# Per-turn interleaving, split first products and an earlier table preload in a chunked RWKV-7 recurrence

## The reference, cut to what matters

```python
def step(state, inp):
    r_t, w_t, k_t, v_t, kk_t, a_t = inp
    sa = jnp.einsum('bhvk,bhk->bhv', state, -kk_t)
    state = (state * w_t[:, :, None, :]
             + sa[..., None] * (kk_t * a_t)[:, :, None, :]
             + v_t[..., None] * k_t[:, :, None, :])
    return state, jnp.einsum('bhvk,bhk->bhv', state, r_t)
...
o = ((o - mean) * lax.rsqrt(var + GN_EPS)).reshape(B_, S, D) * gn_w + gn_b
bonus = jnp.sum(r * k * r_k, axis=-1, keepdims=True) * v
o = (o + bonus.reshape(B_, S, D)) * jax.nn.silu(g)
return o.astype(x.dtype) @ w_o
```

## Time and profile before

| | us |
|---|---|
| median of 3 runs | 2659.07 |
| lowest and highest of them | 2655.52, 2662.23 |
| profiled execution, its own time | 2662.23 |
| its span in the profile | 2660.4 |

### The profile page before, as it was taken

One profiled execution on the slowest core, in us unless ns is written; L12 is line 12 of the kernel. 1 busy time (PEld: TensorE's weight loads), 2 busy tenths in 40 slices (PEclk: granted clock), 3 DMA queues, 4 the chain that ended last, 5 costly groups with the idle time before them and its releaser, 6 DMA issues.

```text
span 2660.4 us, 38077 instructions
## 1 busy us (share of the span) xinstructions
PE 2508.1 (94%) x15424; PEld 2163.3 (81%) x15424; DVE 1568.4 (59%) x2116; ACT 1174.1 (44%) x1547; POOL 71.4 (3%) x92
## 2 busy tenths in 40 slices
PE   7999999998999999999997999999899989998786
PEld 6888888887788888888886888878788878876575
DVE  5888887765656566654446566654516662444455
ACT  5444554644444444443343464643553101444544
POOL 0000000000000000000000000000002110111000
PEclk9999999999999999999999999999999999998898
DMA  6554555554356565565554555545534564222352
GB/s 217 186 190 155 163 173 184 167 185 155 119 182 190 180 191 188 186 191 185 186 183 143 182 162 190 163 135 162 186 98 133 165 194 164 77 73 72 131 167 87
DMA packets 419535, 428.21 MB, mean 161 GB/s; under 512 B 25360, under 2 KB 414480, under 8 KB 418400
## 3 DMA queue, kind: packets, MB, share of 16 engines
q1 hardware_dynamic: 415312, 404.90, 47.8%
q0 software_dynamic: 4048, 20.88, 2.3%
HBM read 415.46 MB, written 10.22 MB: 160 GB/s over the span
## 4 chain that ended last, share of the span: by engine, by line
PE 77%; DVE 13%; ACT 5%; DMA 2%; issue 2%; SPq 0%; POOL 0%; ACTq 0%; DVEq 0%
PE GP L1745 69%; PE SB L1745 7%; DVE wL L982 4%; ACT wH L487 2%; DVE acc L988 1%; DVE y L982 1%; DMA raw<-w_gate_up_dram 1%; DVE j L982 1%; DVE x L982 1%; DVE f L988 0%; DVE ga L982 0%; DMA raw<-w_in_dram 0%; DVE Xs L1448 0%; DVE T L982 0%; DMA gv<-g_keep 0%
## 5 line engine op out<-in xcount | busy, mean ns | idle before, releaser
L982 DVE TENSOR_TENSOR wL<-raw,wH 128x1024 fp32r<-128x1024 f32 x664 | 805.3, 1227 | 618.7 <-ACT wH L487 617.6
L487 ACT CAST wH<-raw 128x1024 fp32r<-128x1024 f32 x664 | 683.9, 1048 | 575.1 <-PE GP L1745 326.1
L1745 PE MATMUL GP<-u2B,wH 128*128 128x512 f32 x1408 | 496.8, 397 | 0.0
L1745 PE MATMUL GP<-uB,wH 128*128 128x512 f32 x1152 | 409.4, 399 | 0.0
L1745 PE MATMUL GP<-u2B,wL 128*128 128x256 f32 x1408 | 398.5, 283 | 10.4 <-DVE u2B L988 8.0
L1745 PE MATMUL GP<-uB,wL 128*128 128x256 f32 x1152 | 329.5, 286 | 15.4 <-DVE wL L982 15.4
L1745 PEld LDWEIGHTS GP<-u2B,wH 128*128 128x128 f32 x1408 | 265.3, 188 | 62.2
L1745 PEld LDWEIGHTS GP<-u2B,wL 128*128 128x128 f32 x1408 | 267.1, 190 | 15.4 <-issue 8.1
L1745 PE MATMUL GP<-xB,wH 128*128 128x512 f32 x768 | 271.4, 395 | 0.0
L1745 PEld LDWEIGHTS GP<-uB,wH 128*128 128x128 f32 x1152 | 217.7, 189 | 52.1
L1745 PE MATMUL GP<-hB,wH 128*128 128x512 f32 x704 | 245.1, 392 | 0.0
(11 more groups left out here) (393 smaller groups left out, 3270.4 us busy)
## 6 DMA issues: line engine op xcount, KB each, us to landing
raw<-w_gate_up_dram SPq DMA_DIRECT2D x352, 256.0 KB, 3.6
raw<-w_in_dram SPq DMA_DIRECT2D x288, 256.0 KB, 3.4
raw<-ev_w_in_dram SPq DMA_DIRECT2D x192, 256.0 KB, 3.3
raw<-w_down_dram SPq DMA_DIRECT2D x176, 256.0 KB, 3.3
raw<-w_out_dram SPq DMA_DIRECT2D x64, 256.0 KB, 3.6
raw<-ev_w_out_dram SPq DMA_DIRECT2D x64, 256.0 KB, 3.3
dw<-w_k_dram SPq DMA_DIRECT2D x64, 256.0 KB, 3.2
dw<-w_r_dram SPq DMA_DIRECT2D x64, 256.0 KB, 3.3
```

Of the source, the lines that this page charges most:

```text
L487: e.copy(wH[SLOT[i]], raw[m % RAW].rearrange("p (k n) -> p k n", k=4)).then_inc(s["hi"], 1)
L982: return e.tensor_tensor(o, a, b, op)
L1745: return e.matmul(o, l, r, start=start, stop=stop, skip_group_check=True)
```

## The change

Three edits are made in four places. The turns are placed one by one: turn t follows the pair at which t / 0.69 is passed, counted anew for every eight units (44 turns each). In a norm on ScalarE the table preload moves from stage 3, ahead of the Ln, to stage 0, ahead of the wait for VectorE and of the Square. In a job's stage 0 on TensorE, eight products of 128 weight columns by 128 moving columns, alternating between the two halves of the partitions, become sixteen of 64 moving columns: for h = 0 four with the 128-wide pair against `rh` and four with `ka` alone (64 wide) against `al`, then the same for h = 1. The product of `be` with `al` is no longer made. In stage 4 the eight products are the same, ordered by h first and then by j.

```diff
         def turns_behind(u):
 
-            t0 = 8 * (u - U0["w_g"])
-            return [3 * (int((t + 1) * FINE / 3) - int(t * FINE / 3)) for t in range(t0, t0 + 8)]
+            t0 = 8 * ((u - U0["w_g"]) % 8)
+            return [int((t + 1) * FINE) - int(t * FINE) for t in range(t0, t0 + 8)]
 
         def turn_at(u):
-            return 3 * int(8 * (u - U0["w_g"]) * FINE / 3)
+            full, t0 = (u - U0["w_g"]) // 8, 8 * ((u - U0["w_g"]) % 8)
+            return full * int(64 * FINE) + int(t0 * FINE)
...
             def norm(k, n, c, h):
                 p0, a0, d0, _ = BASE[k][n]
                 o_, q = rh[:, 8 * h:8 * h + 8, 64 * c:64 * c + 64], fl(sets[k]["M34"].rearrange("p j h t -> p (j h) t"))
+                e.preload_act_table_set("natural_log_exp_and_others")
                 yield
                 e.wait_ge(s[f"jd{k}"], d0 + 1)
                 e.activation(q.rearrange("p (j t) -> p j t", j=8), o_, ACT.Square).then_inc(s[f"ja{k}"], 1)
                 yield
                 yield
-                e.preload_act_table_set("natural_log_exp_and_others")
...
-
-                for j in range(4):
-                    for h, b in enumerate((b0, b1)):
-                        ins = mm(b.rearrange("p (w j t) -> p w j t", w=2, j=4)[:, :, j, :],
-                                 both_[half(h), 4 * (4 * g + j) + c, :], wide[half(h), 5:7, 4 * g + j, cs], True, True)
+                for h, b in enumerate((b0, b1)):
+                    for j in range(4):
+                        mm(b[:, 64 * j:64 * j + 64], both_[half(h), 4 * (4 * g + j) + c, :], rh[half(h), 4 * g + j, cs], True, True)
+                    for j in range(4):
+                        ins = mm(b[up, 256 + 64 * j:320 + 64 * j], ka[half(h), 4 * (4 * g + j) + c, :],
+                                 al[half(h), 4 * g + j, cs], True, True)
                 ins.then_inc(jp, 1)
...
-                for j in range(4):
-                    for h, b in enumerate((b0, b1)):
+                for h, b in enumerate((b0, b1)):
+                    for j in range(4):
                         ins = mm(b[0:64, 64 * j:64 * j + 64], X[half(h), 16 * g + 4 * j + c, :], U0_[half(h), j, :], True, True)
```

## The result

The changed kernel takes 2728.57 us (median of 4 runs, 2722.53 to 2731.47) against 2659.27 us: ratio 1.0259, 95% interval 1.0236 to 1.0281, so about 69 us slower. The forecast was 2711 us with a range up to 2728. The profiled execution took 2725.73 us, with a span of 2723.9, 63.5 more than before.

What follows compares the result with a forecast made beforehand. TensorE bounds the `w_g` stretch (207.8 of 235 us busy). 38.4 stage 0 + 7.5 stage 4 + 8.9 turns + 4.8 preload - 8.0 filled waits = 51.6 us; 2662.2 becomes 2713.8, less 3.2 for the median: 2711 us, range 2686 to 2728.

Steps and rivals of the forecast that it cites:

- the stretch: Stretch of `w_g`, 235 us, the only one the change touches: some 52 us longer, all else the same.
- stage 0: TensorE's products at a job's start: 3.40 us a job against 1.00, so 38.4 us more in 16 jobs.
- One record a step: Stage 0 on TensorE: halves no longer run side by side; steps 0.112 us for 128-wide records, 0.058 for others.
- rival (a): Stage 0: 128-column loads hide behind 64 moving columns, so it costs 23.4 us, not 38.4; time 2696; chance 0.20.
- rival (b): Stages 0 and 4: loads don't overlap with one half at work; steps 0.165 and 0.111 us; time 2751; chance 0.06.
- Rival (c): TensorE: halves still run together and all 22 us of waits go, so not slower: 2660 or 2651; chance 0.06.
- 3.8 us in the last round: ScalarE, round 7: three norms each pay 1.28 us more of table load, nothing hides it, cast 3.8 us later.
- rival (d): ScalarE: the moved preload costs in every round, 12.9 us rather than 1; time 2723; chance 0.06.
- X: Stage 4 on TensorE: eight steps of two records become sixteen of one, 0.47 us a job, 7.5 us in all.
- Masks: TensorE's 13.2 us of waits for VectorE's masks before stage 1's transposes: 3.5 us come back.
- the single turns: Nine more cuts into the `w_g` stream in each of stages 0, 3, 4, 5: 8.9 us; slab-end waits return 4.5.
- the preload: ScalarE: sixteen more table loads, mostly hidden; 1 us in rounds 2 to 6 and 3.8 in round 7, together 4.8.

Runs made afterwards that it cites:

- the doubled run: Changed kernel with stage 0 as the eight old 128 by 128 products, h outer, each done twice: 2710.57 us against 2662.45 for the kernel before, ratio 1.0168.

## Why the prediction was right and wrong

**Right.** The direction, the stretch, and that stage 0 is the main cost. One record a step in each half: in the job at 2397.00 the records with 128-wide loads start 0.112 us apart and the others 0.058. A job takes 3.27 us against the 3.40 forecast, and thus 36.3 us where 38.4 were forecast. The estimate of a load from the slope of the earlier trace rows held against its rival (a) of hidden loads, and rival (b), loads that don't overlap, is refuted by the same 3.27. Rival (c) does not come either: in the change no product of h = 1 starts before the last of h = 0. Its mechanism exists, though, where one shape goes through: there a later half's first records do start ahead of an earlier half's last ones, but it reaches four records only. The sixteen extra table loads, each at its place, and 3.8 us in the last round; rival (d) would have given 12 or more.

**Wrong.** The step that failed is the sum's silence on the clock. Every term was priced at the clock of before, though the earlier trace rows have a granted clock in them and stage 0 was foreseen to take 3.4 us a job on half of the array. The runs showed a fall of the clock inside stage 0 that costs about 21 us net: the forecast rise was 51.6 and the stretch grew by 65.8. Without the fall it would have grown by about 45, so the rest of the sum was some 7 us too high. Its terms: stage 0 2 us too high. X 3 us too high: summed, its records take 14.3 us in the change and 9.8 with single turns alone, 4.5 more where 7.5 were forecast, because of the four records that overlap. Masks 5.7 us too high, where 3.5 us were to come back and 9.2 did. Against them stand the single turns, 12 us alone (7 to 16) where 8.9 less 4.5 were forecast, and the preload, 6 us alone (3 to 9) where 4.8 were. These do not add up to the 7 us, and the intervals are too wide to say why. The range ended at 2728 and missed by half a microsecond, because its upper end held unhidden loads and uncovered waits but no clock. That it missed by so little is luck: terms that were too high made good a third of what the clock cost.

**Open.** That the waits for masks shrink because a longer stage 0 gives VectorE time is read off the waits (17.4 us before, 9.6 with the new stage 0 alone), not tested. Whether the 128-wide loads or the changes of shape bring the fall is open. What the chip looks at when it lowers the clock these runs do not say; they only rank six orders of the same stage.

## What to carry to other kernels

Keep small products of different row halves alternating; then the engine runs them side by side throughout. Keep their shape the same across the switch from one half to the other: then even the wrong order costs little, here 7 us and not 59, since the halves still overlap in four records. Single turns around such a burst add little to that (7.4 us of stage 0 against 5.8). When a burst of small products gets longer, read the granted clock of its stretch as a term of its own, with the price taken from rows at both levels; a TensorE that is busy throughout, as for 100.8 us here, is no sign that the clock is whole. And follow a table load in program order through every function that comes between it and its user: moving it earlier past another function's load does not hide it, it triples it.

## What the runs showed of the hardware that was not expected

The granted clock of TensorE fell to its lower level in and behind bursts of products in which a 128-column load stood ahead of 64 moving columns, on one half of the partitions at a time, with a change of shape between the halves (84 to 87 us of the stretch at 1.2 GHz), although the engine had not waited (busy in all of 100.8 us, clock 0.80). It did not fall in bursts of the same length on one half with 128 moving columns (28 us in the stretch, none in stage 0), nor with the same loads alternating between the halves (2 x 0.04 x 237.8 = 19 us, and 36 in the whole change, none in stage 0).

With one shape, the products of the next half start beside the last four records of the half before, 0.01 us apart, inside a job and between jobs alike. The overlap is four records whether the half has eight or sixteen (the doubled run), and a change of shape between the halves leaves none: the next starts 0.15 us behind.
